# Sample requests of the mixer heads in array groups, the last context products in banks of their own, and two waits moved to their use

## The reference, cut to what matters

```python
def step(s, xs):                       # gated delta rule; a sample request is one chunk of 4 tokens
    q_, k_, u_, w_, g_, a_ = xs
    v_new = u_ - einsum('bhck,bhkv->bhcv', w_, s)
    o = einsum('bhck,bhkv->bhcv', q_ * exp(g_)[..., None], s) + einsum('bhij,bhjv->bhiv', a_, v_new)
    k_dec = k_ * exp(g_last[..., None] - g_)[..., None]
    s = s * exp(g_last)[..., None, None] + einsum('bhck,bhcv->bhkv', k_dec, v_new)
    return s, o
...
probs = softmax(einsum('bthd,bmhd->bhtm', h2 @ w_cq, mem_k) * X_HEAD_DIM ** -0.5)
x = x + einsum('bhtm,bmhd->bthd', probs, mem_v).reshape(b, t, D_MODEL) @ w_co
return rmsnorm(x, norm_final)
```

## Time and profile before

| | us |
|---|---|
| median of 3 runs | 1727.48 (1727.45 to 1730.18) |
| the profiled execution | 1729.08 |
| its span in the trace | 1727.3 |
| PE busy | 1696.4 (98%) |
| DVE busy | 769.5 (45%) |
| ACT busy | 607.9 (35%) |
| POOL busy | 150.4 (9%) |

### The profile page before, as it was taken

How to read it: one execution, slowest core, us unless ns; L and a number is a source line. 1 busy time by engine, 2 the same in 40 slices (tenths; PEclk the granted TensorE clock), 3 DMA queues, 4 the chain that set the end, 5 groups by cost and what they waited for, 6 DMA issues and landing times.

```text
span 1727.3 us, 31514 instructions
## 1 busy us (share of the span) xinstructions
PE 1696.4 (98%) x13184; PEld 1573.8 (91%) x13184; DVE 769.5 (45%) x1301; ACT 607.9 (35%) x984; POOL 150.4 (9%) x163
## 2 busy tenths in 40 slices
PE   6999999999999999999999999999999999999998
PEld 5887899999999999999999999999999986499997
DVE  5676436664755746646334343333121153422222
ACT  5556345244443552443222222223112143322232
POOL 0000001111111121111000011111000000001110
PEclk9999999999999999999999999999999999999998
DMA  7797634243232341432242244445433396533422
GB/s 255 241 293 232 214 91 122 54 113 89 73 88 68 93 112 50 112 99 75 73 108 77 80 118 143 135 125 155 125 97 85 109 392 239 179 93 100 115 82 104
DMA packets 272398, 225.11 MB, mean 130 GB/s; under 512 B 9801, under 2 KB 239058, under 8 KB 266850
## 3 DMA queue, kind: packets, MB, share of 16 engines
q1 hardware_dynamic: 272064, 223.94, 42.7%
q10 hardware_dynamic: 258, 0.09, 0.0%
HBM read 199.07 MB, written 25.30 MB: 130 GB/s over the span
## 4 chain that ended last, share of the span: by engine, by line
PE 96%; issue 1%; DMA 1%; ACT 1%; DVE 1%; POOL 0%; DVEq 0%; SPq 0%; ACTq 0%; POOLq 0%
PE pj L281 64%; PE pj L442 10%; PE pj L2503 3%; PE dk L2171 2%; PE pj L2190 1%; PE dk L361 1%; PE dk L2102 1%; PE pj L2113 1%; PE dk L1713 1%; PE pj L2199 1%; PE dk L1177 1%; PE dk L1183 1%; PE dk L1321 1%; PE dk L1342 1%; PE dk L743 1%
## 5 line engine op out<-in xcount | busy, mean ns | idle before, releaser
L281 PE MATMUL pj<-a_hi,w_high 128*128 128x272 f32 x2432 | 526.4, 298 | 1.8 <-DVE a_lo L2329 1.8
L281 PE MATMUL pj<-a_hi,w_low 128*128 128x272 f32 x2432 | 503.5, 288 | 0.0
L281 PE MATMUL pj<-a_lo,w_high 128*128 128x272 f32 x2432 | 502.1, 288 | 0.0
L281 PEld LDWEIGHTS pj<-a_hi,w_high 128*128 128x128 f32 x2432 | 382.1, 189 | 15.3 <-issue 10.3
L265 DVE TENSOR_TENSOR w_low<-w_raw,w_high 128x2048 fp32r<-128x2048 f32 x96 | 219.8, 2290 | 368.4 <-ACT w_high L255 368.3
L281 PEld LDWEIGHTS pj<-a_lo,w_high 128*128 128x128 f32 x2432 | 382.7, 189 | 0.0
L281 PEld LDWEIGHTS pj<-a_hi,w_low 128*128 128x128 f32 x2432 | 380.4, 189 | 0.1
L255 ACT ACTIVATE w_high<-w_raw 128x2048 fp32r<-128x2048 f32 x96 | 183.4, 1911 | 52.1 <-PE pj L281 44.8
L281 PE MATMUL pj<-mix_hi,w_high 128*128 128x272 f32 x512 | 105.9, 288 | 0.0
L281 PE MATMUL pj<-mix_lo,w_high 128*128 128x272 f32 x512 | 105.4, 288 | 0.0
L281 PE MATMUL pj<-mix_hi,w_low 128*128 128x272 f32 x512 | 105.1, 287 | 0.0
(11 more groups left out here) (406 smaller groups left out, 2040.9 us busy)
## 6 DMA issues: line engine op xcount, KB each, us to landing
w_raw<-in_w_in_dram SPq DMA_DIRECT2D x48, 1024.0 KB, 6.0
w_raw_wide<-in_w_ck_dram SPq DMA_DIRECT2D x16, 1024.0 KB, 6.8
w_raw_wide<-in_w_cv_dram SPq DMA_DIRECT2D x16, 1024.0 KB, 5.9
w_raw<-in_w_out_dram SPq DMA_DIRECT2D x16, 1024.0 KB, 6.2
w_raw<-in_w_cq_dram SPq DMA_DIRECT2D x16, 1024.0 KB, 6.2
w_raw<-in_w_co_dram SPq DMA_DIRECT2D x16, 1024.0 KB, 6.3
xr<-xT_scratch SPq DMA_DIRECT2D x16, 272.0 KB, 6.5
x2T_scratch<-x SPq DMA_DIRECT2D x16, 272.0 KB, 5.6
```

The lines of the kernel that those rows point to most:

```text
L281: mm = pe.matmul(pj[:, 2 * (q % 2) + b, 0:n], wt[:, k, :], x(k, o, n), start=(k == 0 and m == 0), stop=(k == KT - 1 and m == 2))
```

## The change

Four edits.

1. `sample_ks` swaps its operands. The keys and queries of 4 requests, packed by POOL into `kqs` (32 columns: 16 of keys, 16 of queries), are the loaded side, and a state streams with 128 columns; request b writes the 32 partitions of its array column group b % 4, in the half b // 4 of the area. Only 8 of the 32 rows belong to the request. So ACT copies the area (128x256) to `ksv`, and a new step `sample_pick` multiplies it with a constant of ones and zeros, which picks the right rows and turns them. DVE waits for that.
2. `sample_s` uses two row groups: partitions 0 to 31 for four requests and 32 to 63 for the other four. ACT copies `kds` and `vns` to partitions 32 to 63, and POOL makes `vx` as 64x512 in place of 32x1024.
3. The last two context blocks of the last attention head go to `dk[:, 0]` and `dk[:, 1]` with no wait for `cx_low`. The first group of "co" stands outside the loop; it starts at 12 of 16 blocks and waits for 16 after k-step 11 of its first tile.
4. The wait for `xg_ready` 12 stands after the fifth `multiply_half`, no longer ahead of the first.

```diff
@@ constants
-    c[:NS, C_BM:C_BM + NB] = j // NT == np.arange(NB)[None, :]
+    p = np.arange(2 * NS)[:, None]
+    c[:2 * NS, C_BM:C_BM + NB // 2] = p % NS // NT == p // NS * 4 + np.arange(NB // 2)[None, :]
+    p = np.arange(P)[:, None]
+    c[:, C_SEL:C_SEL + NS] = (p % NS == i[:, :NS]) & (p // NS == i[:, :NS] % 16 // NT)
@@ act_delta
             if q == 3:
                 cast()
+                act.wait_ge(ksq_done, 2 * n + 1)
+                act.activation(ksv[:].rearrange("p g n -> p (g n)"), dk[:, 2, 256:512], ACT.Copy).then_inc(ks_taken, 1)
                 rows()
+                act.wait_ge(vns_ready, n + 1)
+                act.activation(vns[NS:2 * NS, :], vns[S_, :], ACT.Copy).then_inc(vns_copied.sem, 1)
...
                 rows()
+                act.wait_ge(kd_ready, n + 1)
+                act.activation(kds[NS:2 * NS, :], kds[S_, :], ACT.Copy).then_inc(kds_copied.sem, 1)
@@ sample_r
-            dve.wait_ge(ksq_done, n + 1)
-            ks = dk[:, 2, 256:320].rearrange("p (b r t) -> p b r t", b=NB, r=2)
...
+            dve.wait_ge(ksq_done, 2 * n + 2)
+            ks = dk[:, 2, 256:320].rearrange("p (g r n) -> p g r n", g=2, r=2)
@@ pool_delta, q == 0
+                pool.wait_ge(qg_ready, n + 1)
+                at_least(pool, ksq_done, 2 * n)
+                pool.tensor_tensor(kqs[:].rearrange("p g (r n) -> p r g n", r=2),
+                                   kq[:, 0:3:2, SEQ:TOK].rearrange("p r (g n) -> p r g n", g=2),
+                                   ones[:, 0:2 * NS].rearrange("p (r g n) -> p r g n", r=2, g=2), ALU.mult).then_inc(kqs_ready, 1)
@@ pool_delta, q == 3
-                pool.wait_ge(ksq_done, n + 1)
+                pool.wait_ge(ksq_done, 2 * n + 1)
...
-                pool.tensor_tensor(vx[S_, :, :], vns[S_, :].unsqueeze(1).to_broadcast([NS, NB, P]),
-                                   cst[S_, C_BM:C_BM + NB].unsqueeze(2).to_broadcast([NS, NB, P]), ALU.mult).then_inc(vx_ready, 1)
+                pool.wait_ge(vns_copied.sem, vns_copied.at(n + 1))
+                pool.tensor_tensor(vx[S2, :, :], vns[S2, :].unsqueeze(1).to_broadcast([2 * NS, NB // 2, P]),
+                                   cst[S2, C_BM:C_BM + NB // 2].unsqueeze(2).to_broadcast([2 * NS, NB // 2, P]),
+                                   ALU.mult).then_inc(vx_ready, 1)
@@ pe_delta
+                pe.wait_ge(kqs_ready, n + 1)
                 for b in range(NB):
-                    mm = pe.matmul(dk[:, 2, 256 + 8 * b:264 + 8 * b].rearrange("p (r t) -> p r t", r=2), s0[:, b, :],
-                                   kq[:, 0:3:2, SEQ + NT * b:SEQ + NT * (b + 1)], start=True, stop=True)
+                    g, a = b // 4, b % 4
+                    mm = pe.matmul(dk[a * NS:(a + 1) * NS, 2, 256 + P * g:256 + P * g + P],
+                                   kqs[:, g, :], s0[:, b, :], start=True, stop=True)
+                mm.then_inc(ksq_done, 1)
+
+            def sample_pick(pe):
+
+                pe.wait_ge(ks_taken, n + 1)
+                for g in range(2):
+                    mm = pe.matmul(dk[:, 2, 256 + NS * g:256 + NS * g + NS], ksv[:, g, :], cst[:, C_SEL:C_SEL + NS],
+                                   start=True, stop=True)
                 mm.then_inc(ksq_done, 1)
...
             def sample_s(pe):
+                pe.wait_ge(kds_copied.sem, kds_copied.at(n + 1))
                 pe.wait_ge(vx_ready, n + 1)
                 for r in range(2):
-                    mm = pe.matmul(dk[:, r, :], kds[S_, :], vx[S_, 4 * r:4 * r + 4, :].rearrange("p b n -> p (b n)"),
-                                   start=True, stop=True)
+                    half = slice(r * NS, (r + 1) * NS)
+                    mm = pe.matmul(dk[:, r, :], kds[half, :], vx[half, :, :].rearrange("p b n -> p (b n)"), start=True, stop=True)
@@ attention
+        def in_dk(h, d):
+
+            return h + 1 == XH and d >= 2
+
+        def context_at(h, d):
+
+            return dk[:, d % 2, :] if in_dk(h, d) else pj[:, 2 + d % 2, :]
...
-                    at_least(pe, cx_low, 4 * h + d - 1)
+                    if not in_dk(h, d):
+                        at_least(pe, cx_low, 4 * h + d - 1)
@@ pe_co
-            pe.wait_ge(cx_low.sem, cx_low.at(16))
-            with pe.Fori(0, 3) as j:
+            pe.wait_ge(cx_low.sem, cx_low.at(12))
+            for q in range(4):
+                multiply(pe, "co", 0, q, tokens(a_hi), tokens(a_lo), TOK,
+                         {11: [lambda pe: pe.wait_ge(cx_low.sem, cx_low.at(16))]} if q == 0 else {})
+            with pe.Fori(1, 3) as j:
                 for q in range(4):
                     multiply(pe, "co", j, q, tokens(a_hi), tokens(a_lo))
-            pe.wait_ge(xg_ready, 12)
             for u in range(4):
                 multiply_half(u, {})
             multiply_half(4, {10: sums(0)})
+            pe.wait_ge(xg_ready, 12)
```

More of the change, by code:

```diff
@@ L69 @@
 C_SSUB, C_BM = C_SINCL + 32, C_SINCL + 64
-C_INV = C_BM + NB
+C_SEL = C_BM + NB // 2
+C_INV = C_SEL + NS
 NCONST = C_INV + NG * 16
@@ L634, in build @@
         fold_at = take.pos[0] - 2 * TOK
+        ksv = put("ksv", [2, P], F32, take.pos[0] - 2 * TOK + 4 * CH * T32)
         own_row = put("own_row", [2, OWN_BANK], F32, take.pos[0] - 2 * TOK)
@@ L638, in build @@
         smp = take("smp", [9, NS])
+        kqs = take("kqs", [2, NS])
         SQ = put("sq", [2, TOK], F32, fold_at)
@@ L659, in build @@
         S_ = slice(0, NS)
+        S2 = slice(0, 2 * NS)
         def per_chunk(x):
@@ L680, in build @@
         tiles_zero = sem("tiles_zero")
+        ks_taken, kqs_ready = sem("ks_taken"), sem("kqs_ready")
+        kds_copied, vns_copied = Reused(squared, 7), Reused(rooted, 7)
         NLEV = LEVELS - L0
@@ L691, in build @@
         sqo, rno = dd[:, 0, :], dd[:, 1, :]
-        vx = put("vx", [NB, P], F32, M_DELTA + 6 * TOK)
+        vx = put("vx", [NB // 2, P], F32, M_DELTA + 6 * TOK)
         def sample3(x):
@@ L1125, in sample_r @@
         def sample_r(dve, n):
[L1127 to L1130 removed]
+            dve.wait_ge(ksq_done, 2 * n + 2)
+            ks = dk[:, 2, 256:320].rearrange("p (g r n) -> p g r n", g=2, r=2)
+            by_half = lambda x: x.rearrange("p (g n) -> p g n", g=2)
+            dve.tensor_tensor(by_half(tmp), ks[:, :, 0, :], by_half(gcb[:, SEQ:TOK]), ALU.mult)
+            dve.tensor_copy(by_half(qs_), ks[:, :, 1, :]).then_inc(rt_step, 1)
             dve.wait_ge(rt_step, 2 * n + 1)
@@ L1353, in pe_delta @@
             return [norms, gram, replicate, turn_v, Tiles(level16_p_wait, level16_p), Tiles(level16_u_wait, level16_u), Tiles(level32_p_wait, level32_p), Tiles(level32_u_wait, level32_u), Tiles(level64_p_wait, level64_p), Tiles(level64_u_wait, level64_u),
-                v_new(0), state_o(0), sample_ks, state_k(1), v_new(1), state_o(1), state_k(2), sample_turn, v_new(2),
+                v_new(0), state_o(0), sample_ks, state_k(1), v_new(1), sample_pick, state_o(1), state_k(2), sample_turn, v_new(2),
                 state_o(2), state_k(3), v_new(3), sample_v, state_o(3), sample_o, sample_s, o_norm]
@@ L2187, in context @@
                 for d in ds:
-                    at_least(pe, cx_low, 4 * h + d - 1)
+                    if not in_dk(h, d):
+                        at_least(pe, cx_low, 4 * h + d - 1)
                     for m in range(2):
-                        mm = pe.matmul(pj[:, 2 + d % 2, :], vtb[h % 2][:, m, d * P:(d + 1) * P], ptb[:, m, :], start=(m == 0), stop=(m == 1))
+                        mm = pe.matmul(context_at(h, d), vtb[h % 2][:, m, d * P:(d + 1) * P], ptb[:, m, :], start=(m == 0), stop=(m == 1))
                     mm.then_inc(cx_done.sem, 1)
@@ L2273, in act_attention @@
                     act.wait_ge(cx_done.sem, cx_done.at(4 * h + d + 1))
-                    act.activation(a_hi[:, DT * h + d, 0:SEQ], pj[:, 2 + d % 2, :], ACT.Copy).then_inc(cx_high.sem, 1)
+                    act.activation(a_hi[:, DT * h + d, 0:SEQ], context_at(h, d), ACT.Copy).then_inc(cx_high.sem, 1)
         def dve_attention(dve):
```

4 lines of the change are left out of this document (1 added, 3 removed), and 2 rows, old and new, of the table PLACE.

## The result

The changed kernel takes 1713.74 us (median of 4 executions, 1713.41 to 1714.20), the kernel before 1727.47 beside it (4 executions, 1726.95 to 1730.18). The ratio is 0.9918, 95% interval 0.9907 to 0.993. The forecast was 1714.0. The profiled execution took 1714.2 us with a span of 1712.4, so the two profiled executions lie 14.9 us apart, and the medians 13.7.

A forecast was written before the change was run, and what follows sets the result against it. PE, busy 98% of the span, was taken as the bound. Heads 5.8, attention and start of "co" 5.1 and tail 2.6 sum to 13.5 us, taken from the 1727.48 median: 1714.0 us, range 1709.5 to 1719.0 (8 in 10).

The forecast's parts named there:

- sample_ks: In each head, sample_ks falls from 1.70 to 0.7 us as four column groups run side by side; bounds 0.6 to 2.0.
- What is late next, v_new(1): After sample_ks, v_new(1) waits for DVE's rr behind the weight split, so 0.76 of 1.0 us is kept.
- The sign as it was written: The changed trace would show PE idle about 0.25 us before v_new(1), put down to rr.
- sample_s: In each head, two row groups side by side take 0.88 us off sample_s's 1.88; bounds 0 and 0.88.
- o_norm: o_norm waits for DVE's addition behind the convolution: 0.32 of 0.88 us kept in seven heads, PE idle about 0.5.
- vx: POOL's vx ends about 621.75, no later than before; if still 1.89 us long, each head loses about 0.2.
- Attention: Waits before the last context blocks and "co" go, with the low clock behind them: 5.1 us, bounds 3.4 and 5.1.
- The clock term of 1.65: Behind the two waits before "co", 3.3 us of work at half clock would run at full clock, saving 1.65.
- The tail: xg_ready wait and low clock before the first half product go; a new 1.1 us w_low wait leaves 2.6 us.
- the next `w_low` comes in time by 0.4: In the tail, after the second half product's wait, the next low weights come 0.4 us early, so 2.6 us stays.
- partial overlap: Rival: array groups overlap only in part; sample_ks takes 1.3 us, total gain 10.1, median 1717.4; chance 0.20.
- The rival with POOL behind DVE: Rival: a delayed vx waits out DVE's convolution, sample_s starts 4.0 us late, median 1739; slower was given 0.04.

The follow-up runs named there:

- the last experiment of the heads: Changed kernel with sample_ks's 8 products reordered so two in a row share a column group; 1714.92 us in one execution.
- second experiment: Kernel before the change with only the two row groups in sample_s, the copies of kds and vns, and vx as 64x512; 1724.71 us, ratio 0.998.
- the first experiment: Kernel before the change with only sample_ks in column groups, ACT's copy and sample_pick; 1723.93 us, ratio 0.9977.

## Why the prediction was right, step by step

- **The sum**: 13.5 forecast, 13.7 between the medians, 14.9 between the profiled executions. It is right in its mechanisms, and its terms miss by up to 1.1 us, partly against each other. That the medians agree to 0.2 is in part luck: the sum was worked out against the profiled execution, where it is 1.4 short, and two of its terms (1.65 each) are clock, which that execution (mean clock 0.995, as only 4 of 28 later ones) had lost and others had not to the same degree. Of the 1.1 us missed in the heads 0.8 lie in the seven periods (5.4 for 4.6) and 0.3 in the last head (1.5 for 1.2).
- **sample_ks**: 0.57 us, forecast 0.7, just under the bounds of 0.6 to 2.0. The price came from the attention's 32 records in four column groups, and the last experiment of the heads shows that the overlap does not hang on the order.
- **What is late next, v_new(1)**: right. `rr` behind the split was named, 0.76 forecast as kept, 0.92 measured (3.50 to 2.58), and 0.29 was given back when the split was moved. The miss of 0.16 is in the release: v_new(1) starts 0.40 us after the start of `rr` (607.39 to 607.79), where 0.48 was taken, and the split itself stands 0.08 us earlier against sample_ks than before. The two records of v_new(1) then take 0.49 in place of 0.38, so the late `rr` costs about 0.2 ahead of v_new(1) (2.58 for 2.37) and 0.1 in it, near the 0.24 that the sum withheld. The sign as it was written did not come: the trace lists no idle time of PE before v_new(1), whose neighbour's recorded end (607.78) reaches up to its start; it is the experiment with the split moved that shows the delay.
- **sample_pick**: 0.43 forecast. Its 4 records start 0.32 after v_new(1) and the step behind it starts 0.37 later (608.48). The copy by ACT that it waits for started at 605.92 and was done 1.8 us before PE asked: covered, as forecast.
- **sample_s**: 0.88 forecast, 0.85 measured with sample_o (2.13 to 1.28). From its own start it is 0.69 (1.88 to 1.19), since it now starts beside the second record of sample_o. The row groups run side by side, as forecast.
- **o_norm**: the addition behind the convolution was named, 0.32 forecast as kept. Alone (second experiment) the period fell by 0.39, and PE lists 0.24 of idle time before o_norm where the prediction's sign had 0.5. The extra comes from `vx`: POOL's op takes 1.03 us in place of 1.89 and no longer overlaps the first op of the convolution, which takes 0.51 in place of 0.68 (below, the kernel before, then the changed one). It took 0.51 with sample_s and `vx` alone too, and 0.68 with sample_ks alone, whose `vx` is the old one. The prediction had a collision of these two among its rivals as a loss; the absence of this one is a gain of 0.17 which the sum did not have. About 0.08 of it is lost again, since the first product behind the wait runs longer (1.16 against 1.08).

```profile
621.57 0.68 DVE L902 TENSOR_SCALAR yq<-ext,hw 128x568 f32<-128x568 f32 x1
```

```profile
618.11 0.51 DVE L911 TENSOR_SCALAR yq<-ext,hw 128x568 f32<-128x568 f32 x1
```

- **vx**: forecast to end at 621.75, no later than before. Set against sample_s it ends 0.6 us ahead of it (617.96 against 618.58), before 0.27. Neither loss came.
- **Attention**: 5.1 forecast and 5.2 measured. The clock term of 1.65 holds for the profiled execution; the first experiment shows that the fall does not come in each one, so the median may have only a part of it. The profiled execution of the kernel before lies 1.6 us above its median, that of the changed kernel 0.5, which is the difference between 14.9 and 13.7; that it is this fall is likely, not shown.
- **The tail**: the step that failed is "the next `w_low` comes in time by 0.4". At the second half product 2.6 us are gained as forecast; at the third 0.45 is lost again, since half(0) of DVE, at 1664.19 before, was there bound by PE's product, and now, 2.6 us earlier, by the arrival of the residual rows. I had moved the whole chain forward without asking what of it comes from a DMA that does not move.
- **The rivals**: partial overlap is refuted by 0.57 us against 1.3 and by the experiment on the order. The Trainium skill ("TensorE: Matmul & The Clock Gate", Part 3: Packing small matmuls) has matmuls start and end in program order and weight loads overlap running matmuls only across row groups, though its own table has three column groups 2.38 times as fast; here 16 records in four column groups with equal rows take a third of the time of 16 over the full width, and records of two steps start out of order. The measurement decides. The rival with POOL behind DVE was not put to the test, since `vx` always came before the convolution.

## What to carry to other kernels

Before a step on the bounding engine is shortened, look at what the next step on it waits for: here two ops of DVE, neither of which hung on the shortened steps, kept 0.76 us a head, as much as the change brought there, and moving them was worth 5.8 us. Where two waits stand in a row, an edit that takes one away may show nothing alone; read the trace and not the median to judge it, then take both away. A gain by clock behind waits belongs in the sum of a profiled execution, with a note that the median may hold only part of it.

## What the runs showed of the hardware

- **POOL works hardly at all while DVE splits.** POOL's scaling of 128x1024 took 3.19 us when it began 0.87 us after the start of DVE's split (606.05, split 605.18 to 607.47), and 1.92 when no split ran beside it, in the kernel with the split moved. It ends 1.77 us behind the split's end in the changed kernel (609.24 and 607.47) and 1.78 in the kernel before (612.31 and 610.53), so of its 1.92 us of work at most 0.15 were done during the split. That agrees with the Trainium skill ("SBUF — State Buffer", SBUF: two separate sides), which calls the port pair of the two engines an exclusive lock held for a whole instruction. It costs both ways: DVE's small product of two operands in SBUF took 0.29 us beside the scaling, and 0.19 when POOL was done or idle.
- **Column groups and row groups are streams of their own** in this kernel: four column groups gain three times (16 records, 1.70 to 0.57 us) though 128 columns are streamed in place of 8, and two row groups take sample_o and sample_s from 2.13 to 1.28 us.
- **The low clock behind two short waits comes in some executions only**: with waits of 1.38 and 1.80 us the clock stayed at 2.4 GHz in one execution, and fell to 1.2 GHz in three others of the kernels shown. Behind a wait of 1.97 us it fell in four of four, and behind the changed kernel's of 0.99 and 0.18 us in none.
- **A wait on PE costs more than its listed idle time**: 0.24 us listed and 0.47 given back when it was taken away, about 0.15 of it, an estimate, since recorded ends lie behind the point at which the next product could start.
